# Decode attention of a hybrid decoder step: turned copies by whole samples, scores in one tiling

## The reference

```python
ckv_past = cache_ckv[layer, page_table].reshape(b, -1, KV_LORA)
kpe_past = cache_kpe[layer, page_table].reshape(b, -1, QK_ROPE)
q_lat = jnp.einsum('bshd,chd->bshc', q_nope, p['w_uk'])
sc_past = jnp.einsum('bshc,btc->bhst', q_lat, ckv_past) + jnp.einsum('bshr,btr->bhst', q_pe, kpe_past)
...
pr = jax.nn.softmax(sc, axis=-1).astype(ckv.dtype)
o_lat = (jnp.einsum('bhst,btc->bshc', pr[..., :n_past], ckv_past)
         + jnp.einsum('bhst,btc->bshc', pr[..., n_past:], ckv))
```

## Time and profile before

| | |
|---|---|
| median of 3 runs | 939.19 us (938.26 to 939.23) |
| the profiled execution | 939.12 us |
| its span, first to last instruction | 937.0 us |
| TensorE busy | 879.6 us, 94% |
| DVE busy | 327.8 us, 35% |
| ACT busy | 199.2 us, 21% |
| DMA, over the span | 347 GB/s mean |
| granted TensorE clock | 0.985 of full |

### The profile page before, as it was taken

How to read it: one execution, slowest core, us unless ns; L and a number is a source line. 1 busy time by engine, 2 the same in 40 slices (tenths; PEclk the granted TensorE clock), 3 DMA queues, 4 the chain that set the end, 5 groups by cost and what they waited for, 6 DMA issues and landing times.

```text
span 937.0 us, 18106 instructions
## 1 busy us (share of the span) xinstructions
PE 879.6 (94%) x7475; PEld 566.4 (60%) x7475; DVE 327.8 (35%) x794; ACT 199.2 (21%) x507; POOL 154.3 (16%) x185
## 2 busy tenths in 40 slices
PE   4999999998899899999899999999999999989897
PEld 3788888876566568746755555554555554545452
DVE  2325570046344498526323212212122122121214
ACT  2000110316123299024111111111011111111012
POOL 0000000032277000000212122121121221212110
PEclk9999999998899899999999999999999999999999
DMA  9966766736499847999899999999999999999994
GB/s 361 399 225 243 291 245 254 285 114 238 147 328 336 327 187 258 414 418 382 336 420 421 418 422 420 418 417 425 417 423 417 421 421 421 420 421 421 420 398 145
DMA packets 61236, 325.46 MB, mean 347 GB/s; under 512 B 16321, under 2 KB 25394, under 8 KB 40610
## 3 DMA queue, kind: packets, MB, share of 16 engines
q1 hardware_dynamic: 47218, 305.53, 81.0%
q0 software_dynamic: 12176, 18.56, 5.9%
q10 hardware_dynamic: 1760, 0.20, 0.2%
HBM read 326.65 MB, written 15.81 MB: 365 GB/s over the span
## 4 chain that ended last, share of the span: by engine, by line
PE 35%; DMA 12%; SPq 2%; DVE 1%; issue 0%; ACT 0%
PE bank L2382 17%; PE bank L2322 9%; PE bank L2333 4%; DMA slot_b<-in_w_e 4%; DMA x<-in_w_e 4%; DMA row_of<-in_w_e 4%; PE bank L2298 2%; SPq L1658 1%; PE bank L2392 1%; PE bank L2368 1%; SPq L1666 1%; DVE slot_b L2704 0%; DVE slot_b L2712 0%; PE bank L2352 0%; ACT slot_b L2533 0%
## 5 line engine op out<-in xcount | busy, mean ns | idle before, releaser
L420 PE MATMUL bank<-h,ring 128*128 128x264 f32 x608 | 138.4, 388 | 0.5 <-PE bank L420 0.3
L420 PEld LDWEIGHTS bank<-h,ring 128*128 128x128 f32 x608 | 114.6, 190 | 21.9 <-issue 2.8
L2606 DVE TENSOR_TENSOR hh<-sge,bank 64x256 f32<-64x256 f32 x64 | 27.1, 423 | 257.3 <-ACT sge L2515 250.2
L1678 POOL DMA_INDIRECT xg<-tok_rows,tab_g x32 | 32.1, 1002 | 331.6 <-PE bank L2298 321.6
L2515 ACT ACTIVATE sge<-bank 64x256 f32<-64x256 f32 x64 | 24.2, 378 | 271.2 <-PE bank L2382 271.2
L2322 PE MATMUL bank<-ring,ht 128*32 128x512 f32 x320 | 72.5, 595 | 8.7 <-DMA x<-in_w_e 4.5
L2382 PE MATMUL bank<-done_out,xt 128*64 128x256 f32 x704 | 78.4, 381 | 0.8 <-DVE ht L2614 0.8
L2382 PE MATMUL bank<-ring,xt 128*64 128x256 f32 x672 | 77.2, 382 | 0.3 <-ACT xt L2506 0.3
L2562 DVE COPY sq<-bank 128x512 f32<-128x512 f32 x64 | 44.2, 691 | 73.3 <-PE bank L2322 73.3
L2382 PEld LDWEIGHTS bank<-done_out,xt 128*64 128x64 f32 x704 | 50.5, 137 | 30.2 <-issue 7.2
L2382 PEld LDWEIGHTS bank<-ring,xt 128*64 128x64 f32 x672 | 46.8, 137 | 34.9 <-issue 14.1
(11 more groups left out here) (489 smaller groups left out, 1303.3 us busy)
## 6 DMA issues: line engine op xcount, KB each, us to landing
ring<-in_w_units SPq DMA_DIRECT2D x25, 2048.0 KB, 11.4
done_out<-in_w_e SPq DMA_DIRECT2D x22, 2048.0 KB
ring<-in_w_e SPq DMA_DIRECT2D x20, 2048.0 KB
slot_b<-in_w_e SPq DMA_DIRECT2D x11, 2048.0 KB
slot_f<-in_w_e SPq DMA_DIRECT2D x10, 2048.0 KB
ring<-in_w_e SPq DMA_DIRECT2D x19, 1024.0 KB
slot_b<-in_w_e SPq DMA_DIRECT2D x10, 1024.0 KB
done_out<-in_w_e SPq DMA_DIRECT2D x10, 1024.0 KB
```

What stands on the lines that cost most here:

```text
L420: mm = pe.matmul(bank[:, t % NB, 0:T], w[:, j, k, :], h[:, k, :], start=(k == 0), stop=(k == KD - 1))
L1678: pool.indirect_dma_start(xg[q % AHEAD][:, :], None, tok_rows, bass.IndirectOffsetOnAxis(ap=tab_g[:, q:q + 1].bitcast(U32), axis=0), bound ...
L2606: dve.tensor_tensor(hh[e % 2][:, :], sg[e % 2][:, :], bank[LB:2 * LB, 4 + e % 2, 0:FE], ALU.mult).then_inc(hh_ready, 1)
```

## The change

`held_turned` becomes `g == 3 or (g >= 1 and b < WIDE)`: samples 2 to 7 all turn 12 pages themselves, 80 in all, and 14 fewer turned copies are loaded. The page buffer of samples 2 and 5 becomes narrower by 256 columns a group; that space goes to two further places for turned pages.

TensorE turns all pages of a sample in one run (`turn_pages`), two pages to a PSUM bank, and ACT and DVE copy a whole bank at a time (128x512) into one of six places (`twos`). Then come the transposes of the probabilities of the sample before, then the scores of all four groups, then `weigh(b - 1)`. The rotary part of the scores is no longer made in 32x32 tiles: `q_rot` has each page's queries in its own 32 columns and zeros elsewhere, so that one 128x32 matmul over all 128 partitions gives the same sums. `q_rot` moves to another place in SBUF, which is in use by weights at the head of the prompt's attention, and is therefore cleared later, between the copies of `q_rows` and `ckv_row`.

```diff
 def held_turned(b, m, g):
-    return g == 3 or (g == 1 and b < WIDE) or (g == 2 and (b < FULL or m % 2 == 0))
+    return g == 3 or (g >= 1 and b < WIDE)
+
+def turns_of(b):
+    return [(m, g) for m in range(NPG // 4) for g in range(4) if not held_turned(b, m, g)]
...
-                            dve.memset(q_rot[:, :, :], 0.0)
                             link(dve.memset(q_lat[:, :, :, :], 0.0))
...
                             dve.tensor_copy(q_rows[:, :], bank[:, 0, :]).then_inc(side_took, 1)
+                            link(dve.memset(q_rot[:, :, :], 0.0))
                             dve.wait_ge(row_done, 1)
...
-                                dve.tensor_copy(q_rot[ROPE * g:ROPE * (g + 1), :, 0:NH], ...)
+                                dve.tensor_copy(q_rot[ROPE * g:ROPE * (g + 1), :, 32 * g:32 * g + NH], ...)
...
+                            def turn_pages(b, twos_of):
+                                for n in twos_of:
+                                    q = FIRST_TWO[b] + n
+                                    if q >= 4:
+                                        pe.wait_ge((turn_took_a, turn_took_d)[q % 2], (q - 4) // 2 + 1)
+                                    for j, (m, g) in enumerate(turns_of(b)[2 * n:2 * n + 2]):
+                                        pe.wait_ge(page_in[b % NBUF][m], 16 * 3 * (b // NBUF + 1))
+                                        for i in range(2):
+                                            at = page_at(b, g) + i * P
+                                            mm = pe.transpose(bank[:, q % 4, (2 * j + i) * P:(2 * j + i + 1) * P],
+                                                              page[b % NBUF][:, m, at:at + P], ident)
+                                    mm.then_inc(turned, 1)
...
                             def score_pages(b):
                                 if b >= 2:
                                     pe.wait_ge(exp5, b - 1)
+                                for m in range(GR):
+                                    pe.wait_ge(page_in[b % NBUF][m], 16 * 3 * (b // NBUF + 1))
+                                    pe.wait_ge(fourth_in[b % NBUF][m], 16 * 2 * (b // NBUF + 1))
+                                    last = max(n for n, (at, _) in enumerate(turns_of(b)) if at == m)
+                                    q = FIRST_TWO[b] + last // 2
+                                    pe.wait_ge(turn_took_a, q // 2 + 1)
+                                    pe.wait_ge(turn_took_d, (q + 1) // 2)
...
+                                    for g in range(4):
+                                        mm = pe.matmul(bank[32 * g:32 * g + 32, 4 + b % 2, m * P:(m + 1) * P],
+                                                       q_rot[:, b, 32 * g:32 * g + 32], rope[b % NBUF][:, m, :],
+                                                       start=False, stop=True)
+                                mm.then_inc(scored, 1)
...
                             for b in range(TS):
                                 if b == 1:
                                     pe.wait_ge(own_took, 1)
+                                turn_pages(b, range(len(turns_of(b)) // 2))
+                                if b:
+                                    turn_weights(b - 1)
                                 score_pages(b)
                                 if b:
                                     weigh(b - 1)
...
+                        def take_pages(eng, copy, b, parity, done, twos_of=None):
+                            for n in range(len(turns_of(b)) // 2) if twos_of is None else twos_of:
+                                q = FIRST_TWO[b] + n
+                                if q % 2 == parity:
+                                    eng.wait_ge(turned, q + 1)
+                                    copy(twos[n], bank[:, q % 4, :]).then_inc(done, 1)
```

More of the change, by code:

```diff
@@ L867, in build @@
                 with ExitStack() as ph:
-                    page_t = early[:, 0:16 * P].rearrange("p (n i t) -> p n i t", n=8, i=2)
+                    twos = [early[:, 4 * P * n:4 * P * (n + 1)] for n in range(4)]
                     free = (U_OS + 1) % RING
@@ L876, in build @@
                     lat = sb("lat", [P, 2, 2, 4, NH], stack=ph)
+                    page_t = sb("page_t", [P, 2, 4 * P], stack=ph)
+                    twos += [page_t[:, n, :] for n in range(2)]
                     assert nc.sbuf_base <= AT_OUT
@@ new lines, in score_pages @@
+                                                at = page_at(b, g) + KVL + i * P
+                                                keys = page[b % NBUF][:, m, at:at + P]
+                                            else:
+                                                n = turns_of(b).index((m, g))
+                                                at = (n % 2 * 2 + i) * P
+                                                keys = twos[n // 2][:, at:at + P]
+                                            pe.matmul(bank[32 * g:32 * g + 32, 4 + b % 2, m * P:(m + 1) * P], q_lat[:, i, b, :], keys,
+                                                      start=(i == 0), stop=False)
@@ L1030, in _ @@
                             mm.then_inc(o5, 1)
-                        def take_pages(eng, copy, b, parity, done, ms=range(NPG // 4)):
-                            for m in ms:
-                                for g in range(4):
-                                    if not held_turned(b, m, g) and TURNS[b, m, g] % 2 == parity:
-                                        n = TURNS[b, m, g]
-                                        eng.wait_ge(turned, n + 1)
-                                        copy(page_t[:, n % 8, :, :], bank[:, n % 4, 0:2 * P].rearrange("p (a c) -> p a c", a=2)).then_inc(done, 1)
+                        def take_pages(eng, copy, b, parity, done, twos_of=None):
[4 more added lines that the diff above has]
+                                    copy(twos[n], bank[:, q % 4, :]).then_inc(done, 1)
                         @block.scalar
```

57 lines of the change are left out of this document (8 added, 49 removed).

## The result

| | before | after |
|---|---|---|
| median | 936.46 us (933.47 to 941.52, 20 runs) | 940.14 us (934.95 to 946.17, 20 runs) |
| the profiled execution, its span | 939.12, 937.0 | 940.47, 938.4 |
| mean granted clock over the timed runs | 0.9875 (129 runs, of every experiment's before) | 0.9840 (20 runs) |

The ratio is 1.0041, with a 95% interval of 1.0026 to 1.0055: slower by 0.4%, where 1% faster was forecast. The run of before that was profiled lies 2.7 us above its median, that of after at its median, so the two traces look nearer to each other than the kernels are.

The account below looks back on a forecast made before the run. DMA engines and TensorE ran level; DMA, at 8.7 us a sample, was to become the bound. Gains 4.0 + 5.7 - 0.3 = 9.4 us took 939.1 to 929.7 us; forecast 927.8 to 933.5, wider range 926 to 936.5.

Parts of the forecast that it names:

- W0 to W6: Decode stage, end of weigh(0) to end of weigh(6): 49.5 us forecast against 55.2 before, 5.7 gained.
- what is late next: Behind a sample's last page stand its transposes and copy, all scores and weigh: 6 us, added to five loads' 43.5.
- L + 6: Slower rival, chance 0.06: least length of two sample periods, L running from load issue at W(b-3), weigh(b-3)'s end, to last page.
- Its 943: Slower rival's time in us at L = 13 with a 1.7 us clock fall each time: 6.9 lost against 2.8 won.
- taken back behind the stage: Rival, chance 0.06: something behind the decode stage has a fixed date, so the gain is lost; about 939 us.
- 7.9 us a sample: TensorE's work per decode sample after the change: 7.9 us, against a period of 9.28 before.
- DMA, per sample: Page loads of samples 3 to 7: 2.88 MB, taken as 8.7 us each, above TensorE's 7.9.
- Samples 0 and 1: Start of decode up to W0: between 3.1 and 4.8 us earlier, 4.0 taken.
- The moved memset: Clearing of q_rot, now on the chain to the second half's probabilities: 0.3 us lost, between 0 and 0.4.
- The clock: Rival, chance 0.16: the clock falls in each sample's run of 28 transposes, 1.7 us each; 938.7 us, or about 934.
- Scores in one tiling, two to a bank: TensorE per sample: 24 transposes in 2.6 us, four groups of scores in 2.7 with no change of tiling between.

Follow-up runs that it names:

- e4: The changed kernel with, from sample 2 on, the last two pairs of turns behind the scores of groups 0 and 1; 935.2 us, ratio 1.0000.
- e7: The changed kernel without loads of pages or rope for samples 3 to 7, computed on old pages; 927.6 us, ratio 0.9890.
- e6: The changed kernel with each group's loads waiting for that group's part of weigh alone; 937.8 us, ratio 1.0018.
- e10: The changed kernel without SP's page loads for samples 3 to 7, GpSimd's loads kept; 934.9 us.
- e2: The kernel before, in its old order, with the changed kernel's loads alone; 936.7 us, ratio 1.0015.
- e1: The changed kernel's order and tiling with the loads of the kernel before; 945.1 us, ratio 1.0108.
- e3: The kernel before with only the zero-padded rope in the scores' tiling and its memset; 934.8 us, ratio 0.9998.
- e16: The changed kernel run again unaltered for a second profile; 941.6 us.
- e14: The split order of e4 with the memset moved into VectorE's idle time; 934.9 us, ratio 0.9996.
- e15: The kernel before with rope in one tiling (e3) and the memset in VectorE's idle time; 935.9 us, ratio 1.0011.
- e17: e14 with fourth chunks of groups 0 and 1 turned on TensorE from sample 2, five pairs ahead of the scores; 934.7 us, ratio 0.9975.
- e8: The changed kernel with weigh(b-1) between the scores of groups 0, 1 and the last two pairs of turns, samples 2 to 6; 939.1 us, ratio 1.0014.
- e9: e4's split order plus loads by group, memset in idle time, weights' transposes behind the two late pairs; 936.3 us, ratio 0.9991.
- e18: e17 with the four transposes of the weights behind the two late pairs instead of the five early ones; 935.7 us, ratio 0.9991.

## Why the prediction was wrong

**The step that failed** is "W0 to W6": that the DMA engines stay saturated, at 8.7 us a sample, and that what is late next adds 6 us once. The rule for it stood among the rivals: the order puts 6 us behind the last page, and two periods cannot be shorter than L + 6. I read L = 11 from before and gave the rival a chance of 0.06. It was 11.7, 12.1, 13.1, 12.6 and 12.5 us from W(b-3) to where TensorE goes on in samples 3 to 7; with 12.6 and the forecast's 6 the rule gives 18.6 us for W3 to W5, and 19.0 was measured. In the forecast's own two terms: from W0 to where TensorE goes on with the last page of sample 7 the trace has 50.1 us, where five loads were put at 43.5, and from there to W6 8.1, where 6 were put (2.1 of it a stop for instructions). The mechanism was named, its size taken from a kernel whose order hid it. Not all of the loss is that rival's, though: by its own arithmetic it decides only from L = 13.4 on without the clock, and L = 12.6 gives 55.8 us for W0 to W6 and still a gain of 2 to 3 us. Its 943 held a fall of the clock in each sample, which did not come, and stops of another kind took its place. e4 (order split, ratio 1.0000) and e7 show the late pages from two sides; e6 agrees.

**The parts of the 58.2 us.** TensorE's own work is 6 x 7.69 = 46.1 (e7; 47.4 was forecast). The five page waits are 5.15 less their pitch, 4.6. The two stops for instructions, 1.75 and 2.11, are 3.7 above the pitch. The remaining 3.8 are small stops in scores and weigh and what follows them, of the kind that e10 ties to GpSimd's loads and gathers. Set against the forecast's 49.5, TensorE's work and the page waits together come to 50.7; the other 7.5 us were in no rival. Since nothing was gained, nothing could be taken back behind the stage. That "TensorE is busy" by 7.9 us a sample did not mean it could be fed in 7.9.

**DMA, per sample.** e4 runs at 8.8 us a sample with the engines at 0.99, near the 8.7 that was forecast. That the engines set this pace is not shown: two of e4's periods are 8.5, and e10, with the engines at 0.60, takes 8.7 too. In after they stood at 0.97 and moved 311 GB/s, not 338.

**Samples 0 and 1.** With the memset 3.7 us were forecast, 2.6 came: from the first transpose of the decode to the last matmul of weigh(0) 3.4 of the 4.0 (15.65 to 12.22), and that transpose comes 0.8 later. The lower clock of the earlier trace rows was gone in both profiles of after, as hoped, but that is not shown to be the new order's doing: it is gone in the three experiments in the old order too. In e2, whose work is that of before up to W0, the stretch takes 14.05 us at the upper level:

```profile
250.00:253.30 3.30, 3.30 (x51) 2.06 (x45) 1.78 (x5) 1.46 (x4) 0.47 (x1) 1.00 0.00 0
```

Both profiles of before so needed 1.6 us more than e2, most of it by the fall of the clock, and against an execution without it the new order gains 1.8 here, not 3.4. The forecast's 4.0 was read from such a profile, while the median it was set against moved from 939.2 (3 runs) to 936.5 (20 runs). What mis-sized the start of the stage is the next term.

**The moved memset.** 0.3 was forecast, with 0.4 as the upper end. The new one is four times as large (128x1024), and is waited for:

```profile
229.62 0.91 DVE L844 MEMSET ring<- 128x1024 f32 x1 [0.16 <-issue]
230.57 0.41 DVE L846 COPY ckv_row<-bank 8x256 f32<-8x256 f32 x1
```

From the start of the copy of `q_rows` to the start of the next copy are 1.79 us here and 0.59 in before: 1.20 more, against the 0.3 that was forecast. In the seven profiles that have one stretch of the lower clock between 226 and 232 there, the way from DVE's first addition of the mask to the first transpose is 21.31 or 21.32 us with it in this place (e1, e3, e10, e16) and 20.10 to 20.12 without (e2, e14, e15): 1.2 us. I had read the diff's line and not the shape behind it.

**The clock.** No fall in the run of transposes itself: 1.00 over the whole stage in after's first profile, so that rival, and with it the rule of the Trainium skill ("TensorE: Matmul & The Clock Gate", Part 4) as its cause, has no support here. But falls behind waits, as in e16, may take part in the result. Within the timed runs of one kernel, a thousandth of mean granted clock goes with 0.50 us; at 0.986, before is at 937.2 (0.3 either way), after at 939.7 (0.7), e4 at 935.6 (1.1), e17 at 935.9 (1.6). Of the 4.2 us between the means of before and after, some 1.7 thus go with the clock, and 2.5 are left for all else, the waits and the memset among it. This is an estimate from what goes together; no run here sets the clock alone.

**Scores in one tiling, two to a bank.** Right in size: 24 transposes in 2.6 us, four groups of scores in 2.56 from first to last start, in after's undisturbed samples and in e7. The gain in TensorE's work is real, and is worth nothing while pages set the pace.

## What to carry to other kernels

Before collecting one engine's work in longer runs, write down for each buffer the loop from its release over the load to its next release, with what stands behind the last landing: the order that is cheapest for the engine can be the one that needs its data earliest. Take the latency of that loop at full queues, not from a kernel whose order hides it. And when idle places are closed, expect smaller ones, fetches and copies, to take over: e8 took the page waits away and exposed copies, and e9 and e18, with the transposes of the weights moved to where TensorE waited, were no faster than e4 and e17.

## What the hardware showed that I had not expected

- TensorE stood up to 2.5 us (3.2 in e1, at instruction 5059) at fixed instructions of the stream, 256 apart or a multiple, until 2.2 to 2.6 us after a 16 KB packet in its instruction queue had started. In e7, with the DMA engines at 0.01, it passed such places without a stop. In e17, where it idled 0.9 us once in each sample for another reason, no such stop was over 0.3 us from sample 2 on.
- After a stop inside a run of 128x32 matmuls the four column strips seem to stay out of step: in e10 four whole weighs take 2.1 to 2.3 us from first to last start, where 1.53 to 1.56 is usual, and matmuls of a weigh start ahead of the last one of the scores before it. In the second row, 30 of a weigh's 32 matmul records take 2.29 us to the end of the last, and all 32 take 1.93 in the earlier trace rows:

```profile
276.34 0.27 PE L963 MATMUL bank<-rope,ring 128*32 128x128 f32 x1
276.51 2.29 PE L982 MATMUL bank<-ring 128*32 128x256 f32 x30
```
